# A wait of TensorE moved by one slot, and a weight load put ahead of a store, in the first stage of a two-block trunk kernel

## What is computed

```python
h = modulate(rmsnorm(x, norm1_g), shift1, scale1)
hc = modulate(rmsnorm(xc, norm1_g), modc[0], modc[1])
q, k, v, rw, gl = jnp.split(h @ w_in, IN_SPLITS, axis=-1)
qc, kc, vc, rwc, glc = jnp.split(hc @ w_in, IN_SPLITS, axis=-1)
...
r_l, v_l, hg_l, kk_l, dirs_l = rwkv_prepare(short_conv(rw, conv_w), decay_w0, decay_w2,
                                           iclr_a0, iclr_a2, k_k, k_a)
...
mem_kv = (mem @ w_mem_kv[layer]).reshape(b, MEM_LEN, 2, N_MEM_HEADS, HEAD_DIM)
```

## Time and profile before

| | us |
|---|---|
| median of 3 runs (1 core) | 3562.92 |
| lowest and highest of them | 3561.78, 3563.11 |
| the profiled execution, its own time | 3547.06 |
| its span, first to last instruction | 3545.3 |
| PE busy in the span | 3257.0 (92%) |
| DVE, ACT, POOL busy | 1899.5, 1156.1, 1559.4 |

### The profile page before, as it was taken

One profiled execution on the slowest core, in us unless ns is written; L12 is line 12 of the kernel. 1 busy time (PEld: TensorE's weight loads), 2 busy tenths in 40 slices (PEclk: granted clock), 3 DMA queues, 4 the chain that ended last, 5 costly groups with the idle time before them and its releaser, 6 DMA issues. The chain is left out here.

```text
span 3545.3 us, 46174 instructions
## 1 busy us (share of the span) xinstructions
PE 3257.0 (92%) x17972; PEld 2580.0 (73%) x17972; DVE 1899.5 (54%) x2664; ACT 1156.1 (33%) x2265; POOL 1559.4 (44%) x1195
## 2 busy tenths in 40 slices
PE   5888999999799999889999999999898999999796
PEld 2666787788598988667788878887675666777565
DVE  3278874545445455587733373337412666564736
ACT  4144441333333333431211021102223665134723
POOL 1114665456144341266666666666551001654432
PEclk8988899999899999999999999999997999999898
DMA  4335555232344342343333333334434321322112
GB/s 168 79 116 149 161 152 180 88 94 70 95 127 108 98 126 62 115 147 89 89 96 95 99 90 97 95 98 105 140 104 118 85 61 40 89 82 60 48 54 78
DMA packets 524317, 358.58 MB, mean 101 GB/s; under 512 B 92497, under 2 KB 477382, under 8 KB 524102
## 3 DMA queue, kind: packets, MB, share of 16 engines
q1 hardware_dynamic: 513446, 325.22, 31.9%
q0 software_dynamic: 4608, 16.78, 1.6%
q10 hardware_dynamic: 6048, 13.63, 1.1%
HBM read 276.85 MB, written 78.18 MB: 100 GB/s over the span
## 5 line engine op out<-in xcount | busy, mean ns | idle before, releaser
L2420 PE MATMUL psum<-place,place 128*128 128x512 f32 x2126 | 862.7, 406 | 82.5 <-POOL place L2398 35.7
L2421 PE MATMUL psum<-place,place 128*128 128x512 f32 x2126 | 842.8, 396 | 0.0
L2422 PE MATMUL psum<-place,place 128*128 128x512 f32 x2126 | 842.0, 396 | 0.0
L2396 POOL CAST place<-place 128x1024 fp32r<-128x1024 f32 (+3 forms) x302 | 303.5, 1005 | 1113.8 <-PE psum L2422 656.7
L2398 POOL TENSOR_TENSOR place<-place,place 128x1024 fp32r<-128x1024 f32 (+3 forms) x302 | 693.2, 2295 | 24.2
L2420 PEld LDWEIGHTS psum<-place,place 128*128 128x128 f32 x2126 | 408.6, 192 | 199.1 <-POOL place L2398 53.8
L2421 PEld LDWEIGHTS psum<-place,place 128*128 128x128 f32 x2126 | 408.8, 192 | 90.8 <-issue 7.5
L2422 PEld LDWEIGHTS psum<-place,place 128*128 128x128 f32 x2126 | 408.0, 192 | 87.9
L662 PE MATMUL psum<-place,place 128*128 128x512 f32 (+1 forms) x712 | 288.0, 405 | 22.3 <-issue 11.6
L663 PE MATMUL psum<-place,place 128*128 128x512 f32 (+1 forms) x712 | 272.8, 383 | 0.0
L664 PE MATMUL psum<-place,place 128*128 128x512 f32 (+1 forms) x712 | 272.4, 383 | 0.0
(11 more groups left out here) (326 smaller groups left out, 5471.8 us busy)
## 6 DMA issues: line engine op xcount, KB each, us to landing
place<-in_w_mlp_up SPq DMA_DIRECT2D x64, 512.0 KB, 4.0
place<-in_w_mlp_down SPq DMA_DIRECT2D x64, 512.0 KB, 4.0
place<-in_w_out SPq DMA_DIRECT2D x48, 512.0 KB, 4.0
chunked<-place SPq DMA_DIRECT2D x64, 320.0 KB, 3.6
place<-in_w_in SPq DMA_DIRECT2D x34, 512.0 KB, 5.7
solve<-in_w_ada POOLq DMA_DIRECT2D x32, 512.0 KB, 6.2
place<-in_lru_w_in SPq DMA_DIRECT2D x32, 512.0 KB, 4.0
place<-in_mla_w_in SPq DMA_DIRECT2D x30, 512.0 KB, 4.2
```

What stands on the lines that cost most here:

```text
L2396: nc.gpsimd.tensor_copy(hi, raw).then_inc(self.w_split, 1)
L2420: pe.matmul(ps, self.w_hi[:, j, k, :], hi, start=(k == 0), stop=False)
L2421: pe.matmul(ps, self.w_hi[:, j, k, :], lo, start=False, stop=False)
L2422: mm = pe.matmul(ps, self.w_lo[:, j, k, :], hi, start=False, stop=(k == kt - 1))
```

## The change

Two places are edited, both in the first stage.

```diff
@@ class Linears, sync @@
         for g, c, n, k0, kn in self.steps:
             if c == 0 and k0 == 0 and g >= 1:
-                store(g - 1)
                 if g + 1 < G:
                     load(g + 1)
+                store(g - 1)
             yield
@@ class Prepare, tensor @@
         yield
+        yield
         pe.wait_ge(self.fixed, 80)
         pe.wait_ge(self.astep, 1)
-        yield
```

## The result

| | before | changed |
|---|---|---|
| first comparison: median (lowest to highest), us | 3557.61 (3535.90 to 3563.11), 7 executions | 3532.43 (3526.40 to 3548.34), 7 |
| second comparison | 3557.66 (3530.74 to 3564.76), 30 | 3530.94 (3526.22 to 3549.54), 7 |
| ratio of the times, 95% interval | | 0.9945 [0.9922, 0.9968]; 0.9935 [0.9912, 0.9958] |
| profiled execution, its own time | 3547.06 | 3532.43 |

The change is faster by 0.55%, some 19.6 us of 3557.6, with an interval from 11.4 to 27.7. Forecast were 10.7 us and 3552.2, with 3545.0 as the lower end of the range.

A forecast was written before the change was run, and what follows sets the result against it. PE bounds most of the first stage, alternating with DVE during Prepare, with POOL taking over in two places; 4.0 + 0 + 2.0 + 4.7 = 10.7 us off the 3562.9 median gives 3552.2 us, range 3545.0 to 3562.0.

The forecast's parts named there:

- The wait, moved: Before z0: piece 14 runs at once, the stall moves to piece 15 behind ACT's copy; 1.8 us gained.
- The load at tile 5: Load leaves the queue ahead of hw and hg, landing 2.2 us earlier; 4.0 us gained at z0 with the moved wait.
- The other loads of Prepare: Earlier POOL splits against DVE's line 857: 2.1 us gained at tile 7, 2.1 lost at tile 11; net 0.
- the third rival: Splits in Prepare fall on DVE where it bounds; six collisions lose 12.2 us, giving 3575.1; chance 0.07.
- The price of 2.1 us: Cost of one collision of POOL's split with DVE's line 857: longest, 2905 ns, against the median, 826 ns.
- the 3.45 us: Possible cost per collision by the shared-port rule: POOL's cast and subtract together could hold DVE up.
- `in_mem`: Start of Window: weight load goes ahead of the store, shortening PE's 2.75 us stall; 2.0 us gained.
- The memory tiles: Of PE's two stalls on POOL's subtract one stays, about 3.05 us; 4.7 us gained of 7.76.
- The sum: Whole kernel: 4.0 + 0 + 2.0 + 4.7 = 10.7 us gained.
- The forecast's base: Median of timed runs, 3562.9 us, from which 10.7 was taken; the profiled execution took 15.86 us less.
- All of it comes off: Rival: clock stays up, Window and memory-tile stalls vanish, no new collision; 19.2 us gained, 3543.8; chance 0.10.
- ACT's queue: Rival: piece 15 waits behind ACT's queue, nothing comes of the loads; 3.8 us gained, 3559.1; chance 0.30.

The follow-up runs named there:

- e7: Changed kernel with ACT's sigmoid and the store of its result one Prepare slot later; median 3527.27 us over 12 executions.
- e3: The kernel before, unedited, run again for a second profile, which ends 12.3 us before the first one of the same kernel.
- e1: Kernel before with only TensorE's wait moved, loads as they stood; median 3554.51 us over 12 executions.
- e2: Kernel before with only the load put ahead of the store, wait as it stood; median 3544.17 us over 12 executions.
- e4: The changed kernel, unedited, run again; in its profile the V tile takes 47.38 us and the first stage ends 7 us later than before's.
- e13: Changed kernel with 4 more matmuls of 512 columns directly ahead of the V tile's first matmul; median 3546.17 us over 12 executions.

## Why the prediction was wrong, point by point

- **The wait, moved: right.** No idle time before piece 14, a new stall before piece 15, released by line 682 right behind the sigmoid (6.07 and 5.80 us; forecast 7.5). e7 shows the queue to be the cause. With the wait alone `z0` comes 2.9 us earlier, forecast 1.8.
- **The load at tile 5: right.** `hw` lands 6.5 to 8.6 us after its issue in the three profiles with the weights ahead of it (before, e3, e1), and 4.7 to 5.2 in those of the changed kernel and e2: 2.3 us on average, against 2.2 taken. `z0` gains 5.3 us instead of 4.0: the clock took 1.43 in place of 2.47 in the first profile, and 2.39 in e4's.
- **The other loads of Prepare, net 0: right in the sum, not in its parts.** From `z0` to the V tile it takes 284.4 and 283.3 us before, 284.8 and 282.0 after. Line 857 with `ends` keeps its median (825 or 826 ns), and its longest is 2852 against 2905 ns. Before has two of these over 2.8 us, at 196.19 and 281.84; the first, beside the split of tile 7, is gone after, as reckoned, and no new one came at tile 11. So the collisions of the third rival did not come. DVE even had less to do: from `z0` to `in_mem` it is busy for 296.3 and 292.5 us in the two profiles of before and 288.9 with the wait alone, but for 282.2 and 283.1 in the changed kernel's and 283.0 with the load alone, with the same instructions. PE's path from `z0` to the V tile gained nothing by it, and why was not followed. The price of 2.1 us was too low for one row: a copy of 128x5 on the same line, 0.17 us at the median, takes 3.07 in before beside POOL's subtract at 411.95, so the prediction's "no case longer than 2.9" does not hold. None reached the 3.45 us that the prediction worked out by the rule that the Trainium skill states on its page "SBUF — State Buffer", section "Who interferes with whom".
- **`in_mem`: oversized.** 2.75 and 2.93 us before, 1.48 and 1.89 after: the stall shrinks by 1.2 us instead of 2.0. Where the tile ran at 1.0 even that is lost ahead of it. From the end of the V tile to `in_mem` it takes 78.7 and 78.6 us before and 79.9 after, as a wait of PE for DVE has grown by 1 us and the granted clock fell from 0.93 to 0.91; in the stretches of before and of the changed kernel these are:

```profile
496.01:574.68 78.67, 72.68 (x332) 56.66 (x333) 35.92 (x41) 28.30 (x72) 54.14 (x73) 0.93 0.61 181
```

```profile
491.17:571.08 79.91, 74.01 (x333) 57.90 (x333) 33.68 (x41) 28.34 (x72) 57.30 (x74) 0.91 0.58 176
```

- **The memory tiles: right in kind, undersized.** One stall of 2.83 us stays (forecast 3.05), and 6.0 us come off instead of 4.7.
- **The sum: right for the path, as far as it can be told.** By the stalls 5.3 + 0 + 1.2 + 6.0 = 12.5, forecast 10.7. With the stretch ahead of `in_mem` in place of its stall it is 5.3 + 0 - 1.3 + 6.0 = 10.0 where the tile ran at 1.0. Between like groups the times differ by 8.2 us (lower, 3537.4 - 3529.2) and 13.1 (upper, 3559.8 - 3546.7), and by 7.9 with V by columns. So the path is worth 8 to 13 us, and the forecast lies inside.
- **The step that failed** is the one behind the sum: "It took 15.86 us less than the median of the timed runs, so I take the difference off the median." That gap is not the same in every execution: its main part is the V tile's clock, which makes the tile 47.38 us long or 31.05. Subtracting from a median assumes that the executions on both sides are alike. Here 17% of before's are in the lower group and 64% of the changed kernel's. Over all executions the means are 3556.0 and 3535.4, 20.6 us apart. Had the share stayed at 26 of 152, the changed kernel's would be 0.171 x 3529.2 + 0.829 x 3546.7 = 3543.7: 12.3 us from the path. The other 8.3 come from the share, a term that the sum did not have. (Reckoned at the changed kernel's share it is 10 and 11.) The median, moreover, jumps across the gap when the share passes one half, which is why the medians differ by 25 to 27. The forecast's base played a part as well: three executions, all of the upper group, gave 3562.92, where seven gave 3557.61, and these 5.3 us are in the 19.8 by which the forecast missed. Why the share moved stays open.
- **The rivals.** "All of it comes off" gave 3543.8 and named the clock, but at the stall before piece 15; the time went beyond it for another reason. ACT's queue did take the wait over, yet the loads paid.

## What to carry to other kernels

A gap between the profiled execution and the median of the runs that is larger than the change you expect has to be explained before any sum is taken off the median: look for a stretch whose length can differ between executions, above all one of small matmuls on a busy TensorE. Compare groups of executions with like groups, and count the share of each as a term of its own. When a wait is moved off an engine, read the queue of the engine that it waits for: here the next wait was two instructions further in ACT's order, and putting one of them later took 6 us more off each group.

## What the runs showed that I had not expected

The granted clock fell from 1.0 to 0.50 inside a tile of 128-column matmuls with no idle time on PE in the profile, in some executions of one and the same program and not in others, and it cost 16.3 us in the tile (47.38 in e4, 31.04 in the changed kernel's first profile). Some 0.9 us of work ahead of the tile (e13) took the share of the good executions from 9 of 14 to 2 of 12 at most. What decides it was not found.
